# A decoder layer with a routed expert stage: a tile's place computed in another position, routing ahead of the count, and the first expert block's list and gather moved into the projection stage

## The chip, the cores and the metric

The kernel runs on one core of a Trainium2 chip (trn2). The metric is the device time of one execution in microseconds, lower is better. TensorE does the matmuls, VectorE, ScalarE and GpSimd (POOL) the elementwise work, SyncE (SP) issues most DMAs. POOL issues the DMAs whose rows are chosen by an index.

## The reference

One layer of a decoder over 2048 tokens of width 1024, in float32. Two groups of attention heads (differential attention, 4 heads; sliding window attention, 8 query heads) give 1024 channels, which one output projection brings back to the residual stream. Then a hierarchical mixture of experts: the token goes to the best of 4 groups, and in it to the best 2 of 8 experts.

```python
x = x + jnp.concatenate([o_diff, o_swa], axis=-1) @ w_out[l]
n2 = rms_norm(x, norm2_g[l])
# router: pg = softmax(n2 @ w_rg + b_rg); el = n2 @ w_re + b_re
# group = argmax(pg); v2, i2 = top_k(el of that group, 2); gates = softmax(v2) * p_top
# every token is listed under its two experts, in order of token; for each block b of an expert e:
#   h = silu(xb @ w_gate[e]) * (xb @ w_up[e]);  y = h @ w_down[e]
x = x + hier_moe(n2, ...)      # gate-weighted sum of the two y
return rms_norm(x, final_g)
```

Experts have a hidden width of 512; there are 32 of them, each with 6 MB of weights.

## The kernel before, in words

The program has five stages, each a block of five instruction streams (one per engine) with a join at its end: input projection, differential attention, window attention, `output_projection` (the block at L1137), and `experts` (L1712). The change touches the last two.

`output_projection` walks over 16 tiles of 128 tokens. Matmuls are made of three passes (high and low parts of both operands, `split_product`, L62 to L64). Two tiles are in flight, in buffers of parity s = t % 2. Each engine's order is written out by hand, and semaphores join them:

* TensorE, tile t: projection of the window heads' half, `turn(t-1)` (transposes of the normed n2, L1450), projection of the other half, `turn_o(t+1)` (L1442), `count(t-2)` (two small matmuls that rank the tokens of a tile within their experts, L1463 and L1464; waits for `choose(t-2)`), `route(t-1)` (logits of 36 columns, L1456).
* VectorE, tile t: `residual` (L1143, waits for the projection), `low_o(t+1)` (L1171), `normalize` (L1151), `sub_norm(t+2)` (L1159, waits for POOL's reciprocal root `orstd`), `low_swa(t+2)` (L1166), `low_w(t-1)` for t from 1 to 8 (L1177, low part of a piece of expert 0's weights), `choose(t-1)` (L1186 to L1213: group and top two experts), `place(t-2)` (L1221 to L1249: rank, slot and gates of each token; at L1244 it waits for ScalarE's two exponentials of that tile).
* ScalarE, tile t: `turned_n2(t-1)` (L1336), `high_o(t+1)` (L1327), the square sum of h (L1365), `square_o(t+2)` (L1315, waits for the load of o_raw), `high_swa(t+2)` (L1323), `high_w(t)` for t below 8 (L1332, waits for the load of a weight piece), `gate_exps(t-2)` (L1344 and L1346).
* POOL, tile t: `rstd` (L1405, L1407), `sub_root(t+2)` (L1383, L1386), `scatter(t-3)` (L1393: two indexed DMAs that write token, gate and place into the list of slots in DRAM).
* SP, tile t: store of h to acc_scratch, loads for tile t+2, a weight piece for t below 8, store of n2 to n_scratch, load of x for t+2. After the last projection SP first issues FIRST_LOADS, six pairs of weight pieces of 1 MB: (expert 0, pairs 4 and 5, the down weights) and (expert 1, pairs 0 to 3), and only then the stores of tile 15.

After the tile loop come `place(14)`, `choose(15)`, `place(15)` and `block_table` (L1254 to L1266: how many blocks each expert has). POOL waits until every scatter has landed.

`experts` starts with a reload of the slot list into SBUF (L1794, L1796), a copy of the first block's 128 token numbers into `fetch` (L1732), and the indexed gather of their n2 rows into `x` (L1736). Meanwhile TensorE spins on 40 dummy transposes (L56, to be warm), turns x (`turn_x(0)`, L1939), spins 16 more, and starts block 0: gate, up, down matmuls (g_ps, u_ps, y_ps). ScalarE and VectorE split expert 0's down weights and then x into high and low parts (L1832, L1886). For each block POOL also fetches rows of `whole` (L1750, first time L1805), which ScalarE squares (L1827) for the final norm. During an expert's last block the next expert's weights are split piece by piece as TensorE is done with a piece, and the loads for the expert after it are issued as the raw pieces come free (`load_pair`, L1599).

The lines around the wait in `place`:

```python
dve.wait_ge(gate_exp, 2 * t + 2)
dve.scalar_tensor_tensor(out=den[:, :], in0=vexp[:, s:s + 1], scalar=1.0, in1=gsum[:, s:s + 1],
                         op0=ALU.add, op1=ALU.mult).then_inc(place_step, 1)
```

Of the kernel before, what the change touches and what calls it, by code (L numbers as in the profile page):

```python
# [7 lines left out]
F32 = mybir.dt.float32  # L8
# [7 lines left out]
P = 128  # L16
D = 1024
# [992 lines left out]
def output_projection(nc, sem, x, o_d, mix_d, wo_hi, wo_lo, wo_raw, wo_split, subln_g, norm2_g, w_rg, b_rg, w_re, b_re,  # L1010
                      ident, power, tables_d, n2_d, acc_d, slots_d, starts, ends, w_d, wg, wu,
                      hi_ready, lo_ready, next_raw, raw_in):
# [9 lines left out]
    with ExitStack() as ctx:  # L1022
# [28 lines left out]
        tri_f = sb("tri_f", [P, P])  # L1051
        consts = sb("consts5", [P, 3, E])
# [40 lines left out]
        spare = proj[:, 0, 1, 0:P]  # L1093
        count_ps = proj[0:E, 1, 1, 0:1]
# [39 lines left out]
        PLACE = 12  # L1134
        PLACED = TILES * PLACE

        with nc.Block() as block:  # L1137
            @block.vector
            def _(dve):
# [111 lines left out]

                def block_table():
# [7 lines left out]
                    dve.wait_ge(counted, TILES + 2)  # L1260
                    dve.tensor_copy(start_row[:, :], start_ps).then_inc(place_step, 1)
# [14 lines left out]
                for t in range(TILES):  # L1276
# [4 lines left out]
                    if t == 0:  # L1281
                        dve.wait_ge(table_in, 32)
                        dve.tensor_copy(tri[:, :], tri_f[:, :])
                        dve.memset(ones[:, :], 1.0)
                        dve.memset(before[:, :, :], 0.0)
# [13 lines left out]
                    if t >= 2:  # L1299
                        place(t - 2, s)  # L1300
                place(LAST - 1, 1 - LAST % 2)
                choose(LAST, LAST % 2)
                place(LAST, LAST % 2)
                block_table()

            @block.scalar
            def _(act):
# [46 lines left out]
                for t in range(TILES):  # L1354
# [23 lines left out]
            @block.gpsimd  # L1378
            def _(pool):

                def sub_root(t, s):
                    pool.wait_ge(oss_ready, t * DK + DK)
                    pool.tensor_tensor(ovar[:, s, :], oss[:, s, :], power[:, 1:2].to_broadcast([P, DK]), ALU.add)\  # L1383
                        .then_inc(ovar_ready, 1)
                    pool.wait_ge(ovar_ready, t + 1)
                    pool.tensor_tensor(orstd[:, s, :], ovar[:, s, :], power[:, 0:1].to_broadcast([P, DK]), ALU.pow)\  # L1386
                        .then_inc(orstd_ready, 1)

                def scatter(t):
# [12 lines left out]
                for t in range(TILES):  # L1402
# [6 lines left out]
                    if t + 2 < TILES:  # L1409
                        sub_root(t + 2, s)  # L1410
# [699 lines left out]
```

## Time and profile before

| what | value |
| --- | --- |
| median of 3 runs | 2266.49 us (2259.28 to 2267.42) |
| the profiled execution's own time | 2252.87 us |
| its span, first to last instruction | 2251.1 us |
| mean granted TensorE clock | 0.968 |
| TensorE busy | 2088.7 us (93% of the span) |
| VectorE busy | 1355.9 us (60%) |
| ScalarE busy | 1145.9 us (51%) |
| GpSimd busy | 733.8 us (33%) |

Times in the rows are microseconds from the start of the span. The output projection's stage runs from about 1052 to 1328, the expert stage from 1328 to the end. PE is TensorE's matmuls, PEld its weight loads, DVE VectorE, ACT ScalarE; L1143 is line 1143 of the kernel before. In brackets stands the engine's idle time just before an instruction and who ended it. Ends of matmuls are modelled.

### The profile page before, as it was taken

What the parts mean: (1) busy time and instruction counts of PE and PEld (TensorE: products, weight loads), DVE (VectorE), ACT (ScalarE), POOL (GpSimd) and SP (SyncE); (2) the same over time, 40 slices, a digit from 0 to 9 for tenths busy, and PEclk for the clock granted to TensorE, in tenths of its full rate; (3) what the DMA queues carried; (4) which work ended last, traced back from release to release, by engine and by line L of the source; (5) the groups of instructions that cost most, each with busy time, mean ns of one, the idle gap of its engine ahead of it and who ended that gap; (6) DMA issues with size and microseconds to landing.
All of it is one profiled execution on the core that took longest, in us unless ns stands there. A gap on an engine that the chain in (4) does not pass through costs nothing. (4 is left out here: it accounts for less than half of the span.)

```text
span 2251.1 us, 40567 instructions
## 1 busy us (share of the span) xinstructions
PE 2088.7 (93%) x12823; PEld 1772.5 (79%) x12824; DVE 1355.9 (60%) x2506; ACT 1145.9 (51%) x2461; POOL 733.8 (33%) x890
## 2 busy tenths in 40 slices
PE   6999999979999994998999959999999999999995
PEld 4888888857777774897878858888888888888884
DVE  5333333339889882764465638857767767685762
ACT  4111111128788882564333328756666666584661
POOL 1111111113434434200132234444444444344443
PEclk9999999989999997998999979999999999999998
DMA  7333333252312106533544369999879978998862
GB/s 211 95 97 98 98 102 102 75 166 67 110 57 85 58 13 153 120 84 99 172 156 158 123 223 300 362 326 303 288 231 315 364 238 288 365 323 269 292 197 68
DMA packets 309528, 408.05 MB, mean 181 GB/s; under 512 B 27056, under 2 KB 221360, under 8 KB 309424
## 3 DMA queue, kind: packets, MB, share of 16 engines
q1 hardware_dynamic: 275504, 333.25, 44.8%
q0 software_dynamic: 30432, 72.19, 12.4%
q10 hardware_dynamic: 3504, 1.51, 0.3%
q8 instruction: 47, 0.77, 0.1%
q14 instruction: 41, 0.34, 0.1%
HBM read 331.83 MB, written 110.94 MB: 197 GB/s over the span
## 5 line engine op out<-in xcount | busy, mean ns | idle before, releaser
L62 PE MATMUL proj<-w_in_lo,n1T_hi 128*128 128x512 f32 (+1 forms) x640 | 245.7, 384 | 14.5 <-DVE w_in_lo L260 14.5
L63 PE MATMUL proj<-w_in_hi,n1T_lo 128*128 128x512 f32 (+1 forms) x640 | 240.0, 375 | 0.0
L64 PE MATMUL proj<-w_in_hi,n1T_hi 128*128 128x512 f32 (+1 forms) x640 | 239.8, 375 | 0.0
L534 ACT ACTIVATE prob<-score,nmax 128x512 f32<-128x512 f32 (+3 forms) x344 | 207.7, 613 | 36.7 <-DVE nmax L620 34.1
L573 POOL TENSOR_SCALAR prob<-prob,scale,lam 128x512 f32<-128x512 f32 (+3 forms) x172 | 147.9, 871 | 229.3 <-DVE scale L636 212.8
L1881 DVE TENSOR_TENSOR wg_lo<-raw_pieces,wg_hi 128x1024 fp32r<-128x1024 f32 x124 | 147.7, 1222 | 103.8 <-ACT wg_hi L1846 103.0
L64 PE MATMUL u_ps<-wu_hi,xT_hi 128*128 128x256 f32 x752 | 210.0, 279 | 0.0
L62 PE MATMUL u_ps<-wu_lo,xT_hi 128*128 128x256 f32 x752 | 209.9, 279 | 0.0
L63 PE MATMUL u_ps<-wu_hi,xT_lo 128*128 128x256 f32 x752 | 209.9, 279 | 0.0
L620 DVE TENSOR_REDUCE nmax<-score 128x2 f32<-128x1024 f32 (+3 forms) x172 | 171.4, 997 | 16.1 <-PE score L664 9.1
L62 PE MATMUL y_ps<-wd_lo,hT_hi 128*128 128x512 f32 x376 | 154.5, 411 | 7.4 <-DVE hT_lo L1892 6.0
L337 POOL TENSOR_TENSOR roped<-roped,cosx 128x512 f32<-128x512 f32 x64 | 70.2, 1097 | 274.8 <-DVE roped L303 274.8
L682 PE MATMUL o_ps<-v_sb,aT 128*128 128x128 f32 x1088 | 153.3, 279 | 5.6 <-ACT o_diff L561 4.3
L1881 DVE TENSOR_TENSOR wd_lo<-raw_pieces,wd_hi 128x1024 fp32r<-128x1024 f32 x128 | 148.3, 1220 | 12.1 <-ACT wd_hi L1868 10.9
L62 PEld LDWEIGHTS proj<-w_in_lo,n1T_hi 128*128 128x128 f32 x640 | 121.5, 190 | 38.1 <-DVE w_in_lo L260 10.5
L64 PE MATMUL y_ps<-wd_hi,hT_hi 128*128 128x512 f32 x376 | 149.6, 398 | 0.0
L63 PE MATMUL y_ps<-wd_hi,hT_lo 128*128 128x512 f32 x376 | 149.6, 398 | 0.0
L62 PE MATMUL g_ps<-wg_lo,xT_hi 128*128 128x512 f32 x376 | 148.7, 395 | 0.0
L63 PE MATMUL g_ps<-wg_hi,xT_lo 128*128 128x512 f32 x376 | 148.5, 395 | 0.0
L64 PE MATMUL g_ps<-wg_hi,xT_hi 128*128 128x512 f32 x376 | 148.5, 395 | 0.0
L212 ACT CAST qkT<-qkt_ps 128x512 fp32r<-128x512 f32 x64 | 32.4, 508 | 225.3 <-PE qkt_ps L382 221.0
L682 PEld LDWEIGHTS o_ps<-v_sb,aT 128*128 128x128 f32 x1088 | 136.6, 193 | 11.3 <-ACT o_diff L561 11.0
(256 smaller groups left out, 5458.2 us busy)
## 6 DMA issues: line engine op xcount, KB each, us to landing
raw_pieces<-in_w_down SPq DMA_DIRECT2D x64, 1024.0 KB
raw_pieces<-in_w_gate SPq DMA_DIRECT2D x62, 1024.0 KB
raw_pieces<-in_w_up SPq DMA_DIRECT2D x62, 1024.0 KB
qk_scratch<-qkT SPq DMA_DIRECT2D x96, 256.0 KB, 2.3
x_sb<-in_x SPq DMA_DIRECT2D x16, 512.0 KB, 4.2
h<-in_x SPq DMA_DIRECT2D x16, 512.0 KB
acc_scratch<-h SPq DMA_DIRECT2D x16, 512.0 KB, 3.0
n_scratch<-n SPq DMA_DIRECT2D x16, 512.0 KB
```

The lines of the kernel that those rows point to most:

```text
L62: pe.matmul(out, hi, w_lo, start=first, stop=False)
L63: pe.matmul(out, lo, w_hi, start=False, stop=False)
L64: return pe.matmul(out, hi, w_hi, start=False, stop=last)
L212: act.copy(qkT[:, b % 2, 0, 0:n, :], qkt_ps[:, b % 2, 0:n, :]).then_inc(qkt_ready, 1)
L337: pool.tensor_tensor(roped[:, s, head:head + heads, :], roped[:, s, head:head + heads, :], cosx[:, n % 2, 0:heads, :], ALU.add).then_inc(r ...
L534: act.activation(prob[:, n % RING, c, 0:w], score[:, n % BUFS, c, 0:w], ACT.Exp, bias=nmax[:, c, n:n + 1], accum_out=part[:, c, n:n + 1]). ...
L573: pool.tensor_scalar(prob[:, u % RING, 1, 0:w], prob[:, u % RING, 1, 0:w], scale[:, 1, u:u + 1], lam[:, 5:6], ALU.mult, ALU.mult).then_inc ...
L620: dve.tensor_reduce(nmax[:, :, n:n + 1], score[:, n % BUFS, :, 0:w], AX.X, ALU.max, negate=True).then_inc(max_ready, 1)
L682: mm = pe.matmul(o_ps[:, :], aT[:, u % 2, b * P:(b + 1) * P], v[:, h, j // P + b, :], start=(u == FIRST[m] and b == 0), stop=(u == LAST[m] ...
L1881: dve.tensor_tensor(piece(LO, k), raw_piece(raw, k), piece(HI, k), ALU.subtract)\
```

## The change

In `output_projection`:

* VectorE does `place(t-2)` right behind `normalize(t)`, ahead of `sub_norm(t+2)`, instead of at the end of the tile, and behind it a new `enlist(t-2)`.
* `enlist` builds the first expert block's list on the chip: `listed[token, row] = token number` where a token's slot is row times LISTED (the first block of expert 0), summed over tiles. A matmul with ones then gives the column of 128 token numbers, which VectorE writes to `fetch`, and POOL gathers `x` at the end of this stage, once all of n2 is stored.
* TensorE does `route(t-1)` ahead of `count(t-2)`; `choose` waits for the count's semaphore instead of the route's (but for the first and last tile), and `route` waits until the logits' buffer has been read.
* ScalarE's queue, not SP's, stores h and n2 of tile 15.
* FIRST_LOADS has four pairs instead of six; pairs 2 and 3 of expert 1 are loaded at the start of `experts`, behind the gather's landing. `gather(0, 0)` goes from there.
* SP loads one more constant table of 128 x 128. The block of TensorE's stream stands ahead of POOL's in the text, with no change of its content but for the above.

```diff
-        PLACE = 12
+        PLACE = 17
...
-                    dve.wait_ge(lg_ready, t + 1)
+                    if t in (0, LAST):
+                        dve.wait_ge(lg_ready, 1 if t == 0 else 2)
+                    else:
+                        dve.wait_ge(counted, t)
...
+                def enlist(t):
+                    base = t * PLACE + 12
+                    dve.wait_ge(place_step, t * PLACE + 9)
+                    dve.tensor_copy(dest_f[:, :], dest[:, t, :]).then_inc(place_step, 1)
+                    dve.wait_ge(place_step, base + 1)
+                    for k in range(TOPK):
+                        dve.scalar_tensor_tensor(out=hit[:, k, :], in0=row0[:, :], scalar=dest_f[:, k:k + 1],
+                                                 in1=consts[:, 2, t:t + 1].to_broadcast([P, P]),
+                                                 op0=ALU.is_equal, op1=ALU.mult).then_inc(place_step, 1)
+                    for k in range(TOPK):
+                        dve.wait_ge(place_step, base + 3 + k)
+                        dve.tensor_tensor(listed[:, :], listed[:, :], hit[:, k, :], ALU.add).then_inc(place_step, 1)
+                    dve.wait_ge(place_step, base + 5)
...
                     dve.wait_ge(counted, TILES + 2)
+                    dve.tensor_scalar(fetch[:, :], listed_ps, 0.0, None, ALU.add).then_inc(fetch_ready, 1)
+                    dve.wait_ge(counted, TILES + 3)
                     dve.tensor_copy(start_row[:, :], start_ps).then_inc(place_step, 1)
...
                     normalize(t, s)
+                    if t >= 2:
+                        place(t - 2, s)
+                        enlist(t - 2)
...
-                    if t >= 2:
-                        place(t - 2, s)
                 place(LAST - 1, 1 - LAST % 2)
+                enlist(LAST - 1)
                 choose(LAST, LAST % 2)
                 place(LAST, LAST % 2)
+                enlist(LAST)
                 block_table()
...
+                    if t == LAST:
+                        act.dma_start(acc_d[t * P:(t + 1) * P, :], h[:, s, :]).then_inc(h_stored[s], 16)
+                act.wait_ge(n2_ready, TILES)
+                act.dma_start(n2_d[LAST * P:TILES * P, :], n2[:, LAST % 2, :]).then_inc(stored[LAST % 2], 16)
...
                 def route(t, s):
                     pe.wait_ge(n2T_ready, t + 1)
+                    if t >= 1:
+                        pe.wait_ge(lg_taken, t)
...
-                    if t >= 2:
-                        count(t - 2, s)
                     if t >= 1:
                         route(t - 1, 1 - s)
+                    if t >= 2:
+                        count(t - 2, s)
...
+                pe.wait_ge(place_step, PLACED)
+                pe.matmul(listed_ps, listed[:, :], ones_f[:, 0:1], start=True, stop=True).then_inc(counted, 1)
...
                 def scatter(t):
-                    pool.wait_ge(place_step, (t + 1) * PLACE)
+                    pool.wait_ge(place_step, t * PLACE + 12)
...
+                for s in range(2):
+                    pool.wait_ge(stored[s], 8 * TILES)
+                pool.wait_ge(fetch_ready, 1)
+                pool.indirect_dma_start(x_first[:, :], None, n2_d,
+                                        bass.IndirectOffsetOnAxis(ap=fetch[:, :], axis=0)).then_inc(x_first_in, 16)
                 pool.wait_ge(scattered, 16 * TOPK * TILES)
...
-FIRST_LOADS = [(0, j) for j in range(EARLY_PIECES // 2, PAIRS)] + [(1, j) for j in range(EARLY_PIECES // 2)]
+FIRST_LOADS = [(0, j) for j in range(EARLY_PIECES // 2, PAIRS)] + [(1, j) for j in range(EARLY_PIECES // 4)]
...
+                sp.wait_ge(x_in, 16)
+                for j in range(EARLY_PIECES // 4, EARLY_PIECES // 2):
+                    load_pair(sp, W_D, raw, raw_in, 1, j)
                 for j in range(EARLY_PIECES // 2, PAIRS):
...
                 pool.wait_ge(own_free, 32)
-                gather(0, 0)
```

## Rows read from the trace of the kernel before

**Rows 1.** The chain of work that ended last, at the first expert block: start, us, what
```profile
1336.33 6.59 DMA x<-n_scratch,fetch
```
**Rows 2.** Who waited for whom, 1060 to 1345: us in total, times, longest us
```profile
PE small_ps L1463 <- DVE later L1228: 7.4, 5, 2.4
```
**Rows 3.** VectorE's timeline (start, us, instruction, idle before): tiles 2, 6, 7, 8
```profile
1102.32 1.22 DVE L1143 TENSOR_TENSOR h<-proj,h 128x1024 f32<-128x1024 f32 x1 [0.41 <-PE proj L64]
...
1167.27 1.23 DVE L1143 TENSOR_TENSOR h<-proj,h 128x1024 f32<-128x1024 f32 x1
...
1176.00 1.14 DVE L1159 SCALAR_TENSOR_TENSOR onorm<-o_raw,orstd,subln_out 128x128 f32<-128x128 f32 x4 [4.02 <-POOL orstd L1386]
...
1181.21 0.19 DVE L1213 TENSOR_TENSOR both<-hot 128x32 bf16<-128x32 f32 x1
...
1182.66 0.15 DVE L1244 SCALAR_TENSOR_TENSOR den<-vexp,gsum 128x1 f32<-128x1 f32 x1
...
1183.04 0.16 DVE L1249 TENSOR_TENSOR pair<-pair,vexp 128x1 f32<-128x1 f32 x1
1183.45 1.23 DVE L1143 TENSOR_TENSOR h<-proj,h 128x1024 f32<-128x1024 f32 x1 [0.25 <-PE proj L64]
...
1199.29 1.23 DVE L1143 TENSOR_TENSOR h<-proj,h 128x1024 f32<-128x1024 f32 x1
```
**Rows 4.** ScalarE's timeline, tile 6
```profile
1176.23 1.05 ACT L1332 CAST wu_hi<-wo_raw 128x1024 fp32r<-128x1024 f32 x1 [1.12 <-DMA wo_raw<-in_w_up]
...
1177.47 0.28 ACT L1346 ACTIVATE vexp<-top 128x1 f32<-128x1 f32 x1
```
**Rows 5.** Timeline of ScalarE and VectorE, tile 13
```profile
1274.90 1.23 DVE L1143 TENSOR_TENSOR h<-proj,h 128x1024 f32<-128x1024 f32 x1
...
1282.71 0.28 ACT L1346 ACTIVATE vexp<-top 128x1 f32<-128x1 f32 x1
...
1283.41 1.14 DVE L1159 SCALAR_TENSOR_TENSOR onorm<-o_raw,orstd,subln_out 128x128 f32<-128x128 f32 x4 [3.79 <-POOL orstd L1386]
...
1289.39 1.23 DVE L1143 TENSOR_TENSOR h<-proj,h 128x1024 f32<-128x1024 f32 x1
```
**Rows 6.** TensorE: a window (length, busy, PEclk, DMA share, GB/s) and its timeline
```profile
1166.00:1177.00 11.00, 10.96 (x45) 9.21 (x46) 5.20 (x17) 3.72 (x12) 2.83 (x5) 0.69 0.67 227
...
1166.04 0.18 PE L1463 MATMUL small_ps<-both,tri 128*128 128x32 bf16 x1 [1.41 <-DVE later L1228]
...
1288.16 0.18 PE L1463 MATMUL small_ps<-both,tri 128*128 128x32 bf16 x1
...
1290.00 0.48 PE L62 MATMUL proj<-wo_lo,mixT_hi 128*128 128x512 f32 x1
```
**Rows 7.** Timeline, the last residual, the last scatter, the next stage's first instruction
```profile
1302.46 1.23 DVE L1143 TENSOR_TENSOR h<-proj,h 128x1024 f32<-128x1024 f32 x1 [3.96 <-PE proj L64]
...
1319.74 0.96 POOL L1393 DMA_INDIRECT slots_scratch<-pair,dest  x1 [0.30 <-issue]
1328.06 0.33 SPq L1715 DMA_DIRECT2D gf_bc<-in_final_g  x1
```
**Rows 8.** A window ahead of the stage change: busy times, PEclk, DMA share, GB/s
```profile
1324.00:1328.00 4.00, 0.00 (x0) 0.00 (x0) 0.00 (x0) 0.00 (x0) 0.00 (x0) 0.50 0.00 0
```
**Rows 9.** Timeline of the expert stage's start
```profile
1328.42 7.52 PE L56 MATMUL y_ps<-ident 128*128 128x128 f32 x40 [9.58 <-PEq L1137]
...
1340.26 1.08 POOL L1805 DMA_INDIRECT whole<-acc_scratch,whole_at  x1 [0.81 <-POOL final_at L1803]
...
1342.96 1.97 PE L1939 MATMUL xT_ps<-ident,x 128*128 128x128 f32 x8 [7.01 <-DMA x<-n_scratch,fetch]
...
1346.02 1.23 DVE L1886 TENSOR_TENSOR xT_lo<-xT_ps,xT_hi 128x1024 fp32r<-128x1024 f32 x1 [10.85 <-ACT xT_hi L1832]
...
1348.00 0.56 PE L62 MATMUL g_ps<-wg_lo,xT_hi 128*128 128x512 f32 x1
...
1350.79 1.06 ACT L1827 ACTIVATE sq<-whole 128x1024 bf16<-128x1024 f32 x1
```

More of the change, by code:

```diff
@@ L1493, in _, with sub_root, scatter @@
                 mm.then_inc(counted, 1)
+                pe.wait_ge(place_step, PLACED)
+                pe.matmul(listed_ps, listed[:, :], ones_f[:, 0:1], start=True, stop=True).then_inc(counted, 1)
                 pe.wait_ge(place_step, PLACED + 3)
                 pe.matmul(start_ps, nb[0:E, :], tri[0:E, 0:E + 1], start=True, stop=True).then_inc(counted, 1)
-            raw = next_raw()
+            raw, x_first = next_raw()
+            @block.gpsimd
+            def _(pool):
+                def sub_root(t, s):
+                    pool.wait_ge(oss_ready, t * DK + DK)
+                    pool.tensor_tensor(ovar[:, s, :], oss[:, s, :], power[:, 1:2].to_broadcast([P, DK]), ALU.add)\
+                        .then_inc(ovar_ready, 1)
+                    pool.wait_ge(ovar_ready, t + 1)
+                    pool.tensor_tensor(orstd[:, s, :], ovar[:, s, :], power[:, 0:1].to_broadcast([P, DK]), ALU.pow)\
+                        .then_inc(orstd_ready, 1)
+                def scatter(t):
+                    pool.wait_ge(place_step, t * PLACE + 12)
+                    pool.wait_ge(placed, 1)
+                    for k in range(TOPK):
+                        pool.indirect_dma_start(slots_d, bass.IndirectOffsetOnAxis(ap=dest[:, t, k:k + 1], axis=0),
+                                                pair[:, t, k, :], None).then_inc(scattered, 16)
+                sub_root(0, 0)
+                sub_root(1, 1)
+                pool.wait_ge(tables_ready, 1)
+                for k in range(TOPK):
+                    ins = pool.tensor_copy(pair[:, :, k, 0].bitcast(I32), tok_i[:, :])
+                ins.then_inc(placed, 1)
+                for t in range(TILES):
+                    s = t % 2
+                    pool.wait_ge(ss_ready, t + 1)
+                    pool.tensor_tensor(var[:, s:s + 1], ss[:, s:s + 1], power[:, 1:2], ALU.add).then_inc(var_ready, 1)
+                    pool.wait_ge(var_ready, t + 1)
+                    pool.tensor_tensor(rstd[:, s:s + 1], var[:, s:s + 1], power[:, 0:1], ALU.pow)\
+                        .then_inc(rstd_ready, 1)
+                    if t + 2 < TILES:
+                        sub_root(t + 2, s)
+                    if t >= 3:
+                        scatter(t - 3)
+                for t in range(LAST - 2, TILES):
+                    scatter(t)
+                for s in range(2):
[3 more added lines that the diff above has]
+                                        bass.IndirectOffsetOnAxis(ap=fetch[:, :], axis=0)).then_inc(x_first_in, 16)
+                pool.wait_ge(scattered, 16 * TOPK * TILES)
+                pool.sem_inc(placed, 1)
@@ L1623, in experts @@
         slots = sb("slots6", [P, LISTED, 3])
-        fetch = sb("fetch6", [P, 1], I32)
         own = sb("own6", [P, 3])
@@ L2043, in build @@
                 raw = []
+                fetch = kept("fetch6", [P, 1], I32)
+                x_in, fetch_ready = sem("p6_x_in"), sem("p6_fetch_ready")
                 def next_raw():
```

71 lines of the change are left out of this document (23 added, 48 removed).

## The prediction

> **What bounds the kernel now.** I read the chain of waits first. In the expert stage it runs block after block on TensorE, and the largest piece that is not TensorE's work is one DMA: the gather of the first block's tokens, 6.59 us [rows 1]. Between the last projection and the first expert block, then, TensorE stands still. The list of TensorE's own waits in the projection stage shows only 7.4 us in five waits, all in front of `count` (L1463) for VectorE [rows 2]. To see who sets the pace of a tile I went to VectorE's timeline.
>
> Call R(t) the start of the residual add (L1143) of tile t. The six tiles t = 2 to 7 take 1199.29 - 1102.32 = 96.97 us, 16.2 each, with tile 6 typical: R = 1167.27, next R = 1183.45 [rows 3]. In tile 6 VectorE idles 4.02 us for the reciprocal roots of the head norm and starts `sub_norm` at R+8.73. From there `sub_norm`, `low_swa`, `low_w` and `choose` run to 1181.40, R+14.13, `place` ends at R+15.9, and the next residual follows. In the late tiles (tile 13, no weight cast) the same chain is 14.49 us: 1274.90 to 1289.39 [rows 5]. From the count's pair of matmuls at 1288.16 to the projection of the next tile at 1290.00 lies `route`, and from there to the residual that the projection releases, 1302.46, are 12.46 us [rows 6, 7]: TensorE needs 14.3 to 14.5. So VectorE's chain, with `place` at its end, sets the pace, and TensorE is only slightly ahead.
>
> **The change, part by part.**
>
> *Place in the gap, tiles 2 to 7.* The gap is 4.02 us and `place` is 1.68 us (1181.44 to 1183.12 [rows 3]), so it would fit. But L1244 in `place` waits for `gate_exps(t-2)`, and on ScalarE that stands behind `square_o`, `high_swa` and, for t below 8, `high_w(t)`, which itself waits 1.12 us for its DMA. In tile 6 the exponential ends at 1177.75, R+10.48 [rows 4], later than the roots that VectorE used to wait for (R+8.73). Behind that wait now stand the rest of `place`, all of `enlist`, `sub_norm` and everything after it.
>
> After the exponential: 0.05 us signal and 0.47 us for den, reciprocal and product (1182.66 to 1183.12 [rows 3]; the next instruction starts 0.08 before the product's 0.16 end). Then `enlist`: one small copy, 0.20; two scalar_tensor_tensor of 128x128, 0.27 each from the row of four in 1.14 us, and 0.08 until the last has landed; two dependent adds of 128x128, 0.30 each, between 0.19 for 32 columns and 1.23 for 1024 [rows 3]. Sum 1.42, with a closing wait 1.43. `enlist` is the unknown operation: I bound it by 0.9 (its five instructions at the small-instruction spacing) and 2.0. So `sub_norm` starts 1.95 us behind the exponential. From there to the end of `choose` is 1181.40 - 1176.00 = 5.40, and 0.04 to the next residual. New tile: 10.48 + 1.95 + 5.44 = 17.87 us. Six tiles: 107.2 against 96.97, **+10.2 us** (+7 to +13.7 by the bounds of `enlist`).
>
> *Late tiles, 8 to 13.* Here the exponential ends at R+8.09 [rows 5]; sub_norm at R+10.04, next residual 5.98 - 1.68 = 4.30 later: 14.34 against 14.49. Six tiles at -0.15, held up at times by TensorE's own work: **-0.8**. VectorE loses as much by the wait as it gains by the gap.
>
> *Route ahead of count.* It covers 1.8 us of each wait for `choose` (1288.16 to 1290.00 [rows 6]). TensorE's 7.4 us [rows 2] go, but in tiles 2 to 7 it waits some 3 us per tile anyway, since VectorE takes 17.87. The added wait for `lg_taken` is over long before. Before the last projection VectorE no longer stands 1.7 us behind TensorE, and count goes after route, so the last tile ends a little sooner: **-0.4** (0 to -1). The 14 dropped signals, the extra 64 KB table, three extra memsets in tile 0 (VectorE idles there) cost nothing; if uncovered, below 1 us together.
>
> *Behind the last residual, T = R(15) = 1302.46.* Before, the last scatter has been issued at 1320.70, T+18.2 [rows 7]. After, `enlist(13)` and `enlist(14)` stand ahead (2.86) and count(14) is waited for (0.4): last issue at T+21.4. The list's own matmul, the fetch column and the gather's issue end at about T+22.7, on POOL behind the scatter. From the last issue to the next stage's first instruction, 1328.06, it is now 7.36 us, of which 4.06 lie after all traffic has ended [rows 7, 8]; the scatter and the store of n2 stand among 6 MB of weights. After, the queues hold 4 MB and are empty by then. So the step costs between 4.1 us (nothing but the tail) and 7.4 (as now); I take 5.0, nearer to the first, since what stood in the queue is gone. Stage start S' = T+26.4 against T+25.6: **+0.8** (-0.1 to +3.2). The two stores moved to ScalarE's queue, some 0.4 us each, are hidden by its wait for the transposes of tile 15; SP's share of them goes.
>
> *First expert block.* Before, TensorE spins 7.52 us, waits for the gather, turns x at half clock in 1.97 us and spins again: the first g matmul is at 1348.00, S+19.94 [rows 9]. After, x has landed before S', so the turn follows the spins at S'+7.9 at full clock (half of 1.97), then ScalarE's cast and VectorE's split, 1344.93 to 1347.25 = 2.32: first matmul at S'+11.25. **-8.7 us.** What is late next is `whole`: POOL issues it some 0.5 us sooner than S+12.2, but now 4 MB of expert 1 are in flight. With a landing like that of rows 1, 6.59 us, it is there 7 us after the first matmul, where ScalarE squares it 2.79 us after (1350.79 [rows 9]). Its casts can catch up in part behind that, so I take a bubble of **+1.5** (0 to +4). The Trainium skill, page "DMA: Bandwidth & Descriptors", section "Anatomy of one DMA — SWDGE (gpsimd) path", gives 2.0 us + bytes/436e3 for such a DMA, 3.2 us for these 512 KB as an estimate; the trace shows twice that while weights are moving, and by the page's figure the bubble would be nil and the total 1.5 us lower.
>
> Sum: 10.2 - 0.8 - 0.4 + 0.8 - 8.7 + 1.5 = **+2.6 us**. The profiled execution itself took 2252.87 us (span 2251.1 and 1.8 around it), so 2255.5; the median of the runs shown is 2266.49, 13.6 above it, and I give the median: **2269.1 us**. A measurement of this kernel tells about 0.5%, 11.3 us, from no change.
>
> **The rivals.**
>
> *A, the gap is used in full (faster).* If the exponentials were early enough, six tiles would fall to what TensorE needs or to the roots: 14.5 us, but 15.5 in one, 88 against 97, and the late tiles lose 3. Then -9 -3.2 -0.4 +0.8 -8.7 +1.5 = -19.0: 2247.5. Against it: order on ScalarE in [rows 4]. It needs an exponential before about R+6.6 (8.5 less 1.95). 0.10.
>
> *B, TensorE's clock (slower).* In tiles 2 to 7 TensorE waits 3 us each. After a wait of 1.41 us the granted clock was 0.69 on average for 11 us [rows 6], which is 3.4 us lost at a level of 1.2 GHz for part of it. TensorE needs 12.5 us from `count` to the next projection's end, and VectorE's tile is 17.87, so it may lose 5.4 us a tile before it decides. At 8 us lost, six tiles cost 15.6 more: total +18, 2284.7. The trace's one such tile speaks against it, three waits in a row for it. 0.12. The Trainium skill, "TensorE: Matmul & The Clock Gate", Part 1, says that an idle array falls to 1.2 GHz and comes back once it is busy; the rows agree, and by it every one of the six tiles would begin slow.
>
> *C, the early gather brings nothing.* If expert 1's weights, `whole` or the stage's end hold the first block, -8.7 turns into about -2: total +9, 2275.5, still within the 0.5%. 0.14. A variant is that TensorE's start only moves a later wait for weights: the loads for the expert after next are triggered by its own use of the pieces, so they move with it, and I hold that for unlikely.
>
> **How the numbers follow.** Forecast 0.64, A 0.10, B 0.12, C 0.14. Forecast and C are no change by the bound; from their upper ends and the enlist bound I move 0.04 to slower. Faster 0.10, same 0.74, slower 0.16. The range: bounds low (enlist 0.9, no bubble, early stage) give -4, high give +11, and the median itself wanders by 4: with part of A and the foot of B, 2256 to 2281.
>
> **What would show it.** VectorE idle ahead of L1244, released by ScalarE's vexp, in tiles 2 to 7, and sub_norm at R+12.4 instead of R+8.7; residual to residual 17.9 there and 14.4 later; `enlist` 1.4 us; stage start 26.4 us after the last residual; x turned 8 us after the stage's start; first g matmul 11.3 after. I am wrong if the tiles 2 to 7 take 16 us or less, if TensorE's clock makes them longer than 18, or if the expert stage grows by what the gather gave.

## The result, and the profile after

The changed kernel takes 2264.49 us (median of 20 runs, 2257.06 to 2272.21), the kernel before beside it 2257.12 us (20 runs). The ratio is 1.0032, with a 95% interval of 1.0019 to 1.0046: some 7 us longer, 4 to 10 by the interval, and within the 0.5% that was called no change. Each kernel was profiled twice. The table cuts the span at the same marks in all four profiles and is worked out from timeline rows. R(t) is the start of the residual add of tile t (L1143 before, L1149 after), the spins are TensorE's first dummy transposes of a stage (L56), and turn_x(1) is the turn of the second block's tokens.

| stretch, us | before | before, again | changed | changed, again |
| --- | --- | --- | --- | --- |
| output projection's spins begin at | 1052.38 | 1054.73 | 1058.49 | 1051.46 |
| to R(0) | 23.02 | 22.93 | 21.89 | 20.31 |
| R(0) to R(2) | 26.92 | 26.92 | 26.78 | 26.78 |
| R(2) to R(8) | 96.97 | 96.34 | 107.69 | 107.73 |
| R(8) to R(15) | 103.17 | 104.44 | 101.17 | 103.94 |
| R(15) to the expert stage's spins | 25.96 | 25.83 | 28.39 | 28.38 |
| spins to first g matmul | 19.58 | 19.95 | 10.18 | 10.10 |
| first g matmul to turn_x(1) | 11.64 | 11.51 | 14.71 | 15.23 |
| turn_x(1) to the end of the span | 891.46 | 893.15 | 888.90 | 894.07 |

From R(0) to turn_x(1), where the changed code acts, it is 284.2 and 285.0 us before, 288.9 and 292.2 after: +5.9 on average. The 6.1 us by which the first profile of the changed kernel began this stage later lie in unchanged stages, and the second profile began it earlier than either profile of the kernel before.

Tile 4 of the changed kernel on VectorE's timeline (columns: start, length, engine, line, operation, output and inputs, count, idle time ahead with its releaser):

```profile
1142.57 1.22 DVE L1149 TENSOR_TENSOR h<-proj,h 128x1024 f32<-128x1024 f32 x1
...
1148.33 0.16 DVE L1250 SCALAR_TENSOR_TENSOR dest<-block,place 128x2 int32<-128x2 int32 x1
1153.06 0.16 DVE L1253 SCALAR_TENSOR_TENSOR den<-vexp,gsum 128x1 f32<-128x1 f32 x1 [4.57 <-ACT vexp L1376]
...
1153.95 0.61 DVE L1267 SCALAR_TENSOR_TENSOR hit<-row,dest_f,consts 128x128 f32<-128x128 f32 x2
1154.60 0.62 DVE L1272 TENSOR_TENSOR listed<-listed,hit 128x128 f32<-128x128 f32 x2
1155.25 1.14 DVE L1165 SCALAR_TENSOR_TENSOR onorm<-o_raw,orstd,subln_out 128x128 f32<-128x128 f32 x4
...
1160.45 0.19 DVE L1222 TENSOR_TENSOR both<-hot 128x32 bf16<-128x32 f32 x1
1160.68 1.22 DVE L1149 TENSOR_TENSOR h<-proj,h 128x1024 f32<-128x1024 f32 x1
```

The same tile on ScalarE's timeline:

```profile
1148.78 0.31 ACT L1345 ACTIVATE osq<-o_raw 128x128 bf16<-128x128 f32 x1 [3.80 <-DMA o_raw<-o_scratch]
...
1151.50 1.05 ACT L1362 CAST wu_hi<-wo_raw 128x1024 fp32r<-128x1024 f32 x1 [0.92 <-DMA wo_raw<-in_w_up]
...
1152.75 0.28 ACT L1376 ACTIVATE vexp<-top 128x1 f32<-128x1 f32 x1
```

Before, VectorE idled about 4 us for the roots and had `sub_norm` at R+8.7 [rows 3]. Now `place` has filled 1.3 us of the gap, and then VectorE stands 4.57 us in front of `den`. The exponential ends at R+10.46 because ScalarE waited 3.80 us for a load and 0.92 for a second. `den` to `sub_norm` is 2.19 us here, 1.96 in most tiles; `sub_norm` starts at R+12.68, the tile takes 18.11. The wait moved from the roots to the exponentials. Over the six tiles of the second profile, VectorE waited 27.8 us for the exponentials and 0.4 us for TensorE (us in all, times, longest):

```profile
DVE den L1253 <- ACT vexp L1376: 27.8, 6, 5.1
...
DVE h L1149 <- PE proj L64: 0.4, 1, 0.4
```

In tile 12, one of the late ones, the wait for the exponentials is short:

```profile
1282.70 0.16 DVE L1253 SCALAR_TENSOR_TENSOR den<-vexp,gsum 128x1 f32<-128x1 f32 x1 [2.32 <-ACT vexp L1376]
...
1288.97 1.22 DVE L1149 TENSOR_TENSOR h<-proj,h 128x1024 f32<-128x1024 f32 x1
```

TensorE over the two stretches (stretch, its length, busy time and count of TensorE, its weight loads, VectorE, ScalarE and POOL, granted clock, DMA share, GB/s), and four matmuls of tile 6:

```profile
1107.16:1214.85 107.69, 98.49 (x482) 81.32 (x480) 66.63 (x252) 36.20 (x103) 21.90 (x34) 0.91 0.43 147
1214.85:1316.02 101.17, 101.17 (x537) 85.18 (x536) 68.93 (x284) 32.27 (x102) 27.67 (x40) 0.98 0.41 136
```

```profile
1180.64 0.63 PE L63 MATMUL proj<-wo_hi,mixT_lo 128*128 128x512 f32 x1
1181.07 0.63 PE L64 MATMUL proj<-wo_hi,mixT_hi 128*128 128x512 f32 x1
...
1186.26 0.40 PE L63 MATMUL proj<-wo_hi,mixT_lo 128*128 128x512 f32 x1
1186.49 0.39 PE L64 MATMUL proj<-wo_hi,mixT_hi 128*128 128x512 f32 x1
```

After two waits (0.87 us ahead of the transposes at L1436 and 1.34 us ahead of `route`) the matmuls start 0.43 us apart, at the 1.2 GHz level, later 0.23 us apart, at 2.4 GHz. The clock did fall: 0.91 on average over the six tiles, against 0.95 over the same tiles before the change.

The end of the stage and the first block, on POOL, SP (the next stage's first instruction), TensorE and ScalarE:

```profile
1336.64 0.96 POOL L1513 DMA_INDIRECT slots_scratch<-pair,dest  x1 [0.30 <-issue]
1338.08 1.00 POOL L1538 DMA_INDIRECT x<-n_scratch,fetch  x1 [0.48 <-issue]
1344.53 0.60 POOL L1839 DMA_DIRECT2D slots<-slots_scratch  x1 [5.45 <-POOLq L1143]
1345.12 0.56 POOL L1841 DMA_DIRECT2D own<-in_empty  x1
...
1353.67 0.95 POOL L1844 MEMSET whole<- 128x1024 f32 x1 [7.02 <-DMA own<-in_empty]
...
1356.61 1.08 POOL L1849 DMA_INDIRECT whole<-acc_scratch,whole_at  x1 [0.84 <-POOL final_at L1847]
```

```profile
1344.07 0.34 SPq L1757 DMA_DIRECT2D gf_bc<-in_final_g  x1
```

```profile
1344.41 6.86 PE L56 MATMUL y_ps<-ident 128*128 128x128 f32 x40 [7.22 <-PEq L1143]
1351.10 1.04 PE L1983 MATMUL xT_ps<-ident,x 128*128 128x128 f32 x8
1351.97 1.91 PE L56 MATMUL y_ps<-ident 128*128 128x128 f32 x16
1354.59 0.49 PE L62 MATMUL g_ps<-wg_lo,xT_hi 128*128 128x512 f32 x1 [0.70 <-DVE xT_lo L1930]
...
1369.03 0.44 PE L1991 MATMUL g_ps<-ident,hid 128*128 128x128 f32 x2 [2.98 <-DVE hid L1949]
```

```profile
1362.95 1.06 ACT L1871 ACTIVATE sq<-whole 128x1024 bf16<-128x1024 f32 x1 [5.54 <-DMA whole<-acc_scratch,whole_at]
```

Against [rows 9] the tokens are there when the 40 spins end, the turn runs at full speed (1.04 us instead of 1.97), and the first g matmul comes 9.6 us sooner behind the stage's start (average of the two pairs). Then ScalarE waits 5.54 us for `whole`, and TensorE 2.98 us for `hid` behind it: that is the block's growth of 3.1 and 3.7 us.

### The profile page after: what moved, and what is told of

Same layout as the page of the kernel before. It is cut to its first block and busy times, and to the rows that moved or that the text cites. A ratio compares the mean times of both kernels' runs of the same rounds, so it can differ in the third digit from the quotient of the medians.

```text
span 2258.2 us, 40657 instructions
## 1 busy us (share of the span) xinstructions
PE 2094.9 (93%) x12825; PEld 1782.1 (79%) x12826; DVE 1377.6 (61%) x2589; ACT 1145.2 (51%) x2461; POOL 734.9 (33%) x889
## 5 line engine op out<-in xcount | busy, mean ns | idle before, releaser
L62 PEld LDWEIGHTS proj<-w_in_lo,n1T_hi 128*128 128x128 f32 x640 | 122.0, 191 | 37.9 <-DVE w_in_lo L260 10.5
```

The lines of the kernel that those rows point to most:

```text
L62: pe.matmul(out, hi, w_lo, start=first, stop=False)
```

## The experiments

The same cuts for every kernel that was run. The ratio is to the kernel before, run beside each of them. "Sum" is R(0) to turn_x(1), 284.2 and 285.0 in the kernel before, 288.9 and 292.2 in the changed one.

| kernel | R(2)-R(8) | R(8)-R(15) | to spins | to g | to turn_x(1) | sum | median, us (runs) | ratio, 95% |
| --- | --- | --- | --- | --- | --- | --- | --- | --- |
| exponentials first | 86.50 | 99.49 | 28.40 | 10.02 | 15.03 | 266.2 | 2241.23 (6) | 0.9925, 0.9899 to 0.9951 |
| place at the end | 105.90 | 110.01 | 28.09 | 9.77 | 15.90 | 296.5 | 2270.70 (10) | 1.0057, 1.0036 to 1.0079 |
| no list | 99.63 | 101.02 | 26.44 | 9.71 | 15.42 | 279.0 | 2253.66 (10) | 0.9976, 0.9957 to 0.9995 |
| all three, slots last | 86.42 | 99.58 | 25.71 | 10.63 | 19.61 | 268.7 | 2246.83 (12) | 0.9951, 0.9934 to 0.9968 |
| gather in next stage | 108.72 | 100.98 | 26.02 | 9.97 | 15.43 | 287.9 | 2265.78 (10) | 1.0027, 1.0014 to 1.0041 |
| own first | 109.00 | 103.33 | 28.21 | 10.55 | 12.11 | 290.0 | 2265.92 (9) | 1.0020, 1.0007 to 1.0034 |
| all three, own first | 89.13 | 100.09 | 25.79 | 9.81 | 11.86 | 263.5 | 2236.53 (6) | 0.9885, 0.9865 to 0.9904 |
| six pairs | 108.04 | 104.62 | 28.34 | 10.40 | 11.96 | 290.1 | 2261.81 (10) | 1.0019, 1.0008 to 1.0029 |
| before + table | 96.96 | 104.65 | 25.95 | 20.20 | 11.61 | 286.3 | 2256.51 (12) | 0.9989, 0.9974 to 1.0003 |
| before + exponentials first | 97.43 | 104.45 | 25.94 | 19.20 | 11.82 | 285.8 | 2261.07 (10) | 1.0000, 0.9981 to 1.0019 |

**1. The exponentials ahead on ScalarE.**

```diff
+                    if t >= 2:
+                        gate_exps(t - 2, s)
                     if t + 2 < TILES:
                         square_o(t + 2, s)
                         high_swa(t + 2, s)
                     if t < EARLY:
                         high_w(t)
-                    if t >= 2:
-                        gate_exps(t - 2, s)
```

> The changed kernel with one thing moved: on ScalarE the two exponentials of tile t-2 stand ahead of square_o, high_swa and high_w instead of behind them. My theory (VectorE's chain waits for the exponentials): vexp ends some 5 us earlier in a tile, the waits of 4.5 to 5.7 us ahead of den go, and VectorE is held next by the reciprocal roots, which come up to 1 us later than before, since square_o now stands behind two exponentials. Then sub_norm starts at about R+9.6 instead of R+12.4, and a tile takes 15.1 us: R(2) to R(8) 90.6 us instead of 107.7, R(8) to R(15) 100 instead of 101.2, the total 17 to 18 us under the changed kernel, about 2247. Rival 1 (the growth is the list's own 1.5 us per tile and a TensorE that runs slower for waiting): R(2) to R(8) stays above 103. Rival 2 (the exponentials only hand over to the roots at once): about 16.2 us a tile, R(2) to R(8) 97, total 10 us less.

The six tiles fell to 86.50 us, 4 less than expected, the total by 23 us. Tile 6 on VectorE and ScalarE, and the windows:

```profile
1163.79 1.22 DVE L1149 TENSOR_TENSOR h<-proj,h 128x1024 f32<-128x1024 f32 x1
...
1169.63 0.15 DVE L1253 SCALAR_TENSOR_TENSOR den<-vexp,gsum 128x1 f32<-128x1 f32 x1
...
1172.51 1.21 DVE L1165 SCALAR_TENSOR_TENSOR onorm<-o_raw,orstd,subln_out 128x128 f32<-128x128 f32 x4 [0.97 <-POOL orstd L1506]
...
1178.02 1.22 DVE L1149 TENSOR_TENSOR h<-proj,h 128x1024 f32<-128x1024 f32 x1
```

```profile
1166.39 0.28 ACT L1376 ACTIVATE vexp<-top 128x1 f32<-128x1 f32 x1
1169.76 0.31 ACT L1345 ACTIVATE osq<-o_raw 128x128 bf16<-128x128 f32 x1 [3.10 <-DMA o_raw<-o_scratch]
```

```profile
1105.74:1192.24 86.50, 86.50 (x477) 73.33 (x475) 66.16 (x253) 36.07 (x103) 29.01 (x34) 1.00 0.54 183
```

The exponential ends at R+2.88 instead of R+10.5. `place` and `enlist` together now fit the gap, with 0.97 us of it left, and `sub_norm` starts at R+8.72, as before the change: the roots are no later, since `square_o` waits for its load anyway (my R+9.6 was too careful). TensorE is busy for all of the stretch at a granted clock of 1.00, and most tiles take its 14.2 to 14.3 us. The 10.7 us that the change lost here, and 10 more, hung on two instructions of 0.28 us in the wrong place.

**2. Place and list back at the end of the tile**, TensorE's order with them.

```diff
-                    if t >= 2:
-                        place(t - 2, s)
-                        enlist(t - 2)
...
                         choose(t - 1, 1 - s)
+                    if t >= 2:
+                        place(t - 2, s)
+                        enlist(t - 2)
...
-                    if t >= 1:
-                        route(t - 1, 1 - s)
                     if t >= 2:
                         count(t - 2, s)
+                    if t >= 1:
+                        route(t - 1, 1 - s)
```

> The changed kernel with place and enlist of tile t-2 back at the end of VectorE's tile (behind choose), and with them TensorE's old order (count ahead of route) and its old signals. The list and the early gather stay. My theory: nothing waits for the exponentials any more, and a tile is the old one plus enlist's 1.49 us: R(2) to R(8) 97.0 + 6 x 1.5 = 106 us, and the late tiles pay too, since there the chain was VectorE's: R(8) to R(15) 103.2 + 6 x 1.5 = 112 at most, TensorE being then the one that waits. The total is then 8 to 9 us above the changed kernel (about 2273). Rival (the place in the gap is what costs; enlist is nearly free because it fits somewhere): R(2) to R(8) 97 to 99, total 5 us or more below the changed kernel.

105.90 and 110.01 us for 106 and at most 112. Tile 6 shows the old wait back, and the list on the path:

```profile
1184.90 1.14 DVE L1165 SCALAR_TENSOR_TENSOR onorm<-o_raw,orstd,subln_out 128x128 f32<-128x128 f32 x4 [3.88 <-POOL orstd L1500]
...
1192.85 0.62 DVE L1269 TENSOR_TENSOR listed<-listed,hit 128x128 f32<-128x128 f32 x2
1193.51 1.23 DVE L1149 TENSOR_TENSOR h<-proj,h 128x1024 f32<-128x1024 f32 x1
```

So with the list, the gap is worth nothing in tiles 2 to 7 (105.9 against 107.7) and 6 to 9 us in the late ones, where the exponentials come at R+8.1. TensorE's order was changed with it, but it played no part that shows: in the late tiles VectorE waited 23.9 us in all for the roots and never for TensorE. The list is what has to be paid for, 1.5 us a tile wherever it isn't in a gap; the total rose by 6 us rather than the expected 8 to 9.

**3. Without the list** (`enlist` is left out, so the first block is computed on token 0's row).

```diff
-        PLACE = 17
+        PLACE = 12
...
                         place(t - 2, s)
-                        enlist(t - 2)
```

> The changed kernel without enlist (its five instructions per tile and its closing wait are left out; the list stays zero, so the first block is computed on token 0's row and the output is not the reference's). Place stays in the gap, route stays ahead of count, the early gather stays. My theory: each of the tiles 2 to 7 loses only enlist's 1.49 us, since the wait for the exponentials stays: R(2) to R(8) 107.7 - 8.9 = 98.8 us, two above the kernel before although place fits the gap. R(8) to R(15): 101.2 less up to 6 x 1.5, but TensorE's own 14.3 a tile is nearly reached, so 99 to 101. The last scatter comes 3 us sooner. Total 2264.5 - 9 - 1 - 3 = about 2251. Rival (the whole growth is enlist): R(2) to R(8) 91 or less, waits for vexp under 1 us.

99.63 us for 98.8. The wait stays at full length without the list, as in tile 5:

```profile
1166.13 0.16 DVE L1253 SCALAR_TENSOR_TENSOR den<-vexp,gsum 128x1 f32<-128x1 f32 x1 [4.59 <-ACT vexp L1373]
...
1166.61 1.14 DVE L1165 SCALAR_TENSOR_TENSOR onorm<-o_raw,orstd,subln_out 128x128 f32<-128x128 f32 x4
```

The growth of 10.7 us thus splits into 8.1 for `enlist` (1.34 a tile) and 2.7 for `place` standing in front of `sub_norm` behind a late exponential (3.3 against the second profile of the kernel before). From R(0) to turn_x(1) this kernel is 9.9 and 13.2 us shorter than the two profiles of the changed one. So in this place the list costs at least the 9.6 us that it brings in the first block; in the gap of experiment 1 it costs nothing in tiles 2 to 7, where TensorE was busy throughout.

**4. The kernel before, with only ScalarE's order changed** (the diff of experiment 1 on the kernel before).

> The kernel before, with only ScalarE's two exponentials of tile t-2 ahead of square_o, high_swa and high_w. My theory: place stands at the end of VectorE's tile there and its exponentials are long done, so taking them earlier brings nothing by itself; the roots are not later either, since square_o waits for its load for longer than the 0.5 us that the exponentials take. R(2) to R(8) 96 to 98 us, the ratio to the kernel before 1.000 within 0.2%. Rival (ScalarE's order has a gain of its own, whatever VectorE does): R(2) to R(8) under 94, ratio 0.997 or less.

It took 97.43 us for 96 to 98, at a ratio of 1.0000. Early exponentials are worth nothing by themselves, and 21 us where `place` stands in the gap (107.7 to 86.5).

**5. The first gather in the next stage.**

```diff
-                for s in range(2):
-                    pool.wait_ge(stored[s], 8 * TILES)
-                pool.wait_ge(fetch_ready, 1)
-                pool.indirect_dma_start(x_first[:, :], None, n2_d,
-                                        bass.IndirectOffsetOnAxis(ap=fetch[:, :], axis=0)).then_inc(x_first_in, 16)
                 pool.wait_ge(scattered, 16 * TOPK * TILES)
...
+                pool.wait_ge(fetch_ready, 1)
+                pool.indirect_dma_start(x[:, :], None, n2_d,
+                                        bass.IndirectOffsetOnAxis(ap=fetch[:, :], axis=0)).then_inc(x_in, 16)
                 pool.dma_start(slots[:, :, :].rearrange("p b c -> p (b c)"),
```

> The changed kernel with one DMA moved: the gather of the first block's tokens is POOL's first instruction of the expert stage instead of its last of the projection stage; the list and fetch stay. My theory: the join waited for the gather's landing through POOL's drain, which took 4.98 us after the change and 2.67 before. So the stage starts 2.3 us sooner behind the last residual (25.6 to 26 instead of 28.05), and the tokens, issued 0.7 us into the stage, land under TensorE's spins: first g matmul at S'+10.5 to 11.5. Total 2 us below the changed kernel. Rival (the drain has nothing to do with it, and the issue on POOL is merely moved): stage start at 27 or later, first g matmul at S'+12 or later, total the same or above.

```profile
1340.64 0.96 POOL L1513 DMA_INDIRECT slots_scratch<-pair,dest  x1 [0.30 <-issue]
1346.45 0.98 POOL L1835 DMA_INDIRECT x<-n_scratch,fetch  x1 [4.85 <-POOLq L1143]
```

```profile
1345.76 0.34 SPq L1752 DMA_DIRECT2D gf_bc<-in_final_g  x1
```

```profile
1352.56 1.09 PE L1981 MATMUL xT_ps<-ident,x 128*128 128x128 f32 x8 [0.20 <-DMA x<-n_scratch,fetch]
```

The stage's spins start 26.02 us behind R(15), 2.4 sooner, and TensorE waits 0.20 us for the tokens: the 9.6 us of the first block stay. From the end of the last scatter's issue (1341.60) to the stage's first instruction it is 4.2 us, and POOL's drain ahead of the join is back at 2.67 us. What the early gather gives is the list (tokens that need no reload of the slots), not the stage in which it is issued. The 2 us expected of the whole kernel don't show: 1.0027 and 1.0032 can't be told apart.

**6. POOL's preparations in another order, twice.** First with the slots behind the gather of `whole`, together with edits 1 and 5:

```diff
-                pool.dma_start(slots[:, :, :].rearrange("p b c -> p (b c)"),
-                               slots_d.rearrange("(p b) c -> p (b c)", p=P)).then_inc(own_free, 16)
                 pool.dma_start(own[:, :], empty_d.rearrange("(p b) c -> p b c", p=P)[:, 0, :]).then_inc(own_free, 16)
-                pool.memset(y[:, :], 0.0).then_inc(y_ready, 1)
-                pool.wait_ge(own_free, 32)
                 pool.memset(whole[:, :], 0.0).then_inc(at_ready, 1)
                 pool.memset(final[:, :], 0.0).then_inc(at_ready, 1)
+                pool.wait_ge(own_free, 16)
...
+                pool.dma_start(slots[:, :, :].rearrange("p b c -> p (b c)"),
+                               slots_d.rearrange("(p b) c -> p (b c)", p=P)).then_inc(slots_in, 16)
+                pool.memset(y[:, :], 0.0).then_inc(y_ready, 1)
+                pool.wait_ge(slots_in, 16)
```

> Three edits on the changed kernel together: the exponentials ahead on ScalarE (as in the run of that alone), the gather of the first block's tokens issued as POOL's first instruction of the expert stage instead of the last of the projection stage, and POOL's preparations of the expert stage reordered so that the gather of whole comes ahead of the reload of the slots. My theory: -17.5 from the tiles 2 to 8; the stage's join no longer waits for the gather through POOL's drain, -2.3, while the tokens still land about when TensorE's spins end, so the first g matmul stays at S'+10.5 to 12; the bubble of 3.1 us behind the first block's matmuls goes. Sum -22, total about 2242.5, which is below both kernels. Rival: TensorE gets back the time later (loads of weights become the bound), total above 2250.

```profile
1319.91 1.07 POOL L1845 DMA_INDIRECT whole<-acc_scratch,whole_at  x1 [0.84 <-POOL final_at L1843]
...
1322.32 0.59 POOL L1849 DMA_DIRECT2D slots<-slots_scratch  x1
...
1334.64 0.18 POOL L1773 COPY fetch<-slots 128x1 int32 x1 [10.77 <-issue]
```

`whole` comes in time, but the slots now stand behind it; POOL waits 10.77 us for them with the root of the final norm queued behind, and the stretch grows to 19.61 us. At 2246.83 us for the expected 2242.5 this was below both kernels, yet not below experiment 1 (2241.23): the new order on POOL cost more than it brought. Then the slots right behind `own`, ahead of the wait, alone and with edits 1 and 5:

```diff
+                pool.dma_start(own[:, :], empty_d.rearrange("(p b) c -> p b c", p=P)[:, 0, :]).then_inc(own_free, 16)
                 pool.dma_start(slots[:, :, :].rearrange("p b c -> p (b c)"),
-                               slots_d.rearrange("(p b) c -> p (b c)", p=P)).then_inc(own_free, 16)
-                pool.dma_start(own[:, :], empty_d.rearrange("(p b) c -> p b c", p=P)[:, 0, :]).then_inc(own_free, 16)
-                pool.memset(y[:, :], 0.0).then_inc(y_ready, 1)
-                pool.wait_ge(own_free, 32)
+                               slots_d.rearrange("(p b) c -> p (b c)", p=P)).then_inc(slots_in, 16)
                 pool.memset(whole[:, :], 0.0).then_inc(at_ready, 1)
                 pool.memset(final[:, :], 0.0).then_inc(at_ready, 1)
+                pool.wait_ge(own_free, 16)
...
+                pool.memset(y[:, :], 0.0).then_inc(y_ready, 1)
+                pool.wait_ge(slots_in, 16)
```

> The changed kernel with POOL's preparations of the expert stage in another order: the load of own ahead of the reload of the slots, each on a semaphore of its own, the memsets of whole and final in the wait, and the gather of whole as soon as own is there; then the memset of y and only then the wait for the slots. My theory: the 3.1 us by which the first block grew against the kernel before (first g matmul to turn_x(1): 14.71 against 11.64 us) are ScalarE's wait for whole. Whole is issued at about S'+8 instead of S'+12.5 and lands at S'+14.5, ScalarE's wait of 5.54 us ahead of sq shrinks under 2, and the stretch is 11.6 to 12.5 us: total 2.5 to 3 below the changed kernel. An earlier order, in which the slots came behind the gather of whole, moved the wait onto the slots and made that stretch 19.6 us; here they go ahead of it. Rival (the bubble is TensorE's or the weights'): the stretch stays at 14 to 15.

> Exponentials ahead on ScalarE, the first gather as POOL's first instruction of the expert stage, and own, slots, whole in that order (the last two edits are also run alone beside it). My theory: 86.5 us from R(2) to R(8), stage start 25.7 behind the last residual, first g matmul S'+10.6, then 12 to turn_x(1): 21 - 0.7 for the late tiles - 2.4 - 2.7 = 26.8 below the changed kernel's profile in these stretches, total about 2237, 5 below the kernel with the exponentials alone (2241.2). Rival (a later wait takes the savings of the first block): the same as with the exponentials alone, 2241 or more.

```profile
1363.22 1.06 ACT L1873 ACTIVATE sq<-whole 128x1024 bf16<-128x1024 f32 x1 [2.96 <-DMA whole<-acc_scratch,whole_at]
```

Alone, first g matmul to turn_x(1) falls to 12.11 us, as expected, though ScalarE's wait only falls to 2.96 us and not under 2; the total of 2265.92 us doesn't show the 2.5 to 3 us. Together the stretch is 11.86 us. The last kernel takes 2236.53 us for an expected 2237, the fastest of all: 27 us less than the changed kernel by the sums of the table, 28 by the medians, 1.15% under the kernel before (0.96 to 1.35). Against experiment 1 alone it is 2.8 us by the sums, with 2.6 us more in tiles 2 to 7 (89.13 against 86.50), where the two kernels have the same program. The intervals of the two ratios overlap, so that it is faster than experiment 1 is not shown.

**7. Six pairs of weights ahead, as in the kernel before.**

```diff
-FIRST_LOADS = [(0, j) for j in range(EARLY_PIECES // 2, PAIRS)] + [(1, j) for j in range(EARLY_PIECES // 4)]
+FIRST_LOADS = [(0, j) for j in range(EARLY_PIECES // 2, PAIRS)] + [(1, j) for j in range(EARLY_PIECES // 2)]
...
-                sp.wait_ge(x_in, 16)
-                for j in range(EARLY_PIECES // 4, EARLY_PIECES // 2):
-                    load_pair(sp, W_D, raw, raw_in, 1, j)
```

> The changed kernel with FIRST_LOADS of six pairs (6 MB) as in the kernel before, so no load of expert 1 waits for the gather of the first tokens. Theory: the early gather, the stores of tile 15 and the last scatters then stand among 6 MB of weights. The gather needs both stores of n2 first; it lands 1 to 5 us later, and since the join waits for it through POOL's drain, the stage starts 1 to 5 us later than T+28.05. The total is 0 to 4 us above the changed kernel. Rival (the queues don't matter for the gather): stage start at T+28, and the total falls by 0 to 2 us since expert 1's weights are there sooner.

The rival was right: the spins begin at 28.34 us, not later, and the bubble is gone (11.96 us):

```profile
1353.21 0.56 POOL L1838 DMA_DIRECT2D own<-in_empty  x1
...
1360.02 0.95 POOL L1841 MEMSET whole<- 128x1024 f32 x1 [5.29 <-DMA own<-in_empty]
...
1362.97 1.08 POOL L1846 DMA_INDIRECT whole<-acc_scratch,whole_at  x1 [0.84 <-POOL final_at L1844]
```

```profile
1366.68 1.06 ACT L1868 ACTIVATE sq<-whole 128x1024 bf16<-128x1024 f32 x1 [0.95 <-DMA whole<-acc_scratch,whole_at]
```

`own` is there 6.8 us after its issue instead of 8.5, `whole` 3.7 us after its own instead of 6.3. In the changed kernel the two pairs that are held back until the tokens are there move right beside these two loads, and without them there the bubble is gone. The total, 1.0019, is in line with it, though its interval overlaps that of the changed kernel.

**8. What lies in the unchanged stages.** The kernel before with only the third table (64 KB of constants, not read); the kernel before again; the changed kernel again.

```diff
-    tables = [r[:, None] < r[None, :], values]
+    tables = [r[:, None] < r[None, :], values, np.broadcast_to(r * LISTED, (P, P))]
```

> The kernel before, with nothing but the third table of constants (64 KB more in DRAM, not read). It asks whether the 6.1 us by which the changed kernel's output projection begins later, in front of any changed stage, come with the program's data. Theory (spread of executions): the ratio to the kernel before is 1.000 within 0.2%, and the stage begins anywhere between 1052 and 1058. Rival (placement in DRAM shifts something in the unchanged stages): ratio 1.0025 or more, stage start at 1057 to 1059.

> The kernel before, unchanged, for a second profile of it. If the output projection begins within 1054 to 1058 us here, the 6.1 us by which the changed kernel's began later than in the first profile (1052.4) are the spread of executions. If it begins at 1052 to 1053 again, with all profiles of changed kernels above it, the change moves something in the unchanged stages. In either case R(0) to R(2) is 26.8 to 26.9 us, R(2) to R(8) 97 within 1, R(8) to R(15) 103 within 1.

> The changed kernel again, for a second profile of it. The three profiles of kernels with the old program order began the output projection at 1052.4, 1054.7 and 1055.1 us, the nine with the new one between 1053.1 and 1061.6, 57.9 on average. If it begins below 1056 here, a part of the 6.1 us of the first comparison is shown to be spread. R(2) to R(8) is 107.7 within 1.5, stage start 28 behind the last residual, first g matmul 10.5 behind that.

The table costs nothing that shows (0.9989). The output projection began at 1055.07 with the table, at 1054.73 and 1051.46 in the second profiles, and at 1059.21 in the kernel before with exponentials first. So either program order has both early and late starts, and the 6.1 us of the first comparison are no cost of the change; a shift of 1 or 2 us under this spread can't be excluded. The late tiles spread too: kernels with the old order took 103.2 to 104.7 us for R(8) to R(15).

## Why the prediction was right, point by point

It gave no change within 0.5%, and that holds. Its time of 2269.1 us was 4.6 above the measured 2264.5, for two reasons of opposite sign: the median of three runs it stood on, 2266.49, was 9.4 above the median of twenty, and the net growth was 7.4 us by the medians (5.9 by the stretches) where the sum said 2.6, just outside the interval of 4 to 10. That the two errors partly cancel is luck. The terms below are averages of two profiles each, unless it says otherwise.

* **Place in the gap, tiles 2 to 7: +10.2 forecast, +11.1 measured** (10.7 by the first pair of profiles). The step that carried the forecast, that place's wait at the exponentials takes the place of the wait for the roots, is shown by experiments 1, 3 and 4. `enlist` was put at 1.43 us and is 1.49 between its copy and `sub_norm`; the tile at 17.87, and nine of the twelve measured 17.65 to 18.48.
* **Late tiles and last tile: -1.2 forecast, -1.3 measured** (103.8 to 102.6), inside a spread of as much. That place gains 0.15 us a tile here can't be shown; that it keeps the list from costing 1.5 a tile is shown by experiment 2.
* **End of the stage: +0.8 forecast, +2.5 measured.** The issue of the last scatter ended at T+21.6 (forecast T+21.4). From there to the next stage's first instruction at 1344.07 it was 6.5 us, where I had put 5.0 (it had been 7.4 before). The premise that the queues are empty by then held: the last scatter landed at 1338.63, 1.0 us after its issue, and no weights moved. What failed is the gather's term: I had priced its issue and not its landing. POOL's drain, the instruction ahead of the join, took 2.67 us before the change and 4.98 after; with the gather moved out of the stage (experiment 5) it is 2.67 again, and the 6.5 us are 4.2, the "nothing but the tail" that I had as the lower bound.
* **First expert block: -8.7 forecast, -9.6 measured.** The turn at full clock and the split behind it were as worked out, and 0.9 us quicker in all.
* **The bubble for `whole`: +1.5 forecast, +3.1 and +3.7 measured.** The mechanism was right, its size was not: I had `whole` issued 0.5 us sooner than before, and it was issued 0.3 later (12.5 us into the stage) because the small load of `own` took 8.5 us among the weights, and the casts queued behind ScalarE's wait could not catch up as assumed. Experiments 6 and 7 take the bubble away from two sides, by an earlier `whole` and by no weights beside it.
* **Rival A** (the gap used in full, 2247.5) was 0.10 and did not come, but it priced what was missing: its condition, an exponential before R+6.6, is what experiment 1 supplies, at 2241.
* **Rival B** (TensorE's clock) did not come, though the clock fell, to 0.91 in tiles 2 to 7. In tile 6 twelve matmuls at 0.43 instead of 0.23 us cost 2.4 us, and TensorE ran from one count to the next with 0.16 us of idle time. But VectorE waited 0.4 us for TensorE over the six tiles, and with early exponentials the clock was 1.00. Nor did every one of the six tiles begin slow, as I had worked out: tile 2 ran at a granted clock of 1.00 in both profiles, and the other five had a mean of 0.80 to 0.96. TensorE also waited for `lg_taken`, which I had called over long before: 4.4 us in four waits (4.6 in the second profile), at no cost, since VectorE set the pace.
* **Rival C** did not come: nothing of the first block's gain is given back behind turn_x(1) (891.5 and 893.2 before, 888.9 and 894.1 after).

## What to carry to other kernels

A gap in a timeline is the wait of the instruction that stands behind it. The work that is put into it brings waits of its own: before it is moved, look up when every one of its inputs is ready, and move the producers too. Here `place` in the gap was worth 2 us less than nothing in tiles 2 to 7 (107.7 against 105.9), early exponentials alone nothing, and the two together 19 us (105.9 to 86.5). The gather issued last in a stage was paid for at the join (2.4 us), and a load that is held back "until there is room" should not land beside a small load that others wait for: here that was the bubble of 3 us.

## What the runs showed of the hardware

* The gather of `whole` (128 rows of 4 KB) landed 3.7 us after its issue in experiment 7, where the weight loads were ending (DMA share 0.40 from issue to landing), and 6.2 to 8.2 us after it in the kernels with 4 MB of weights in flight. The formula in the Trainium skill, page "DMA: Bandwidth & Descriptors", section "Anatomy of one DMA — SWDGE (gpsimd) path", gives 3.2 us as an estimate for 512 KB: experiment 7 comes within half a microsecond of it, and the loaded cases take 1.9 to 2.6 times as much. The first gather of `x`, as large, took 4.3 us in both profiles of the changed kernel (1338.08 to 1342.42), with no other traffic: a third more than the estimate.
* The 1.5 KB load of `own` took 5.0 to 9.0 us among other traffic, longer than the 4.3 us of a gather of 512 KB that had the queues to itself.
* GpSimd's drain at the end of the stage follows the gather, though no semaphore of that stage asks for it. In the seven traces with the gather in this stage the drain lasts 4.36 to 5.23 us and ends 1.4 us behind the gather's landing (1343.83 and 1342.42 in the changed kernel). In the traces without it, experiment 5 among them, it is 2.67 us each time. Whether other DMAs of POOL hold it as well was not tried.
